# A decoder block on one core: gather by transposed matmuls in halves, branch pieces in another order, refills and stores by halves

## The chip, the cores and the metric

The program runs on one NeuronCore of a Trainium2 chip. The metric is the device time of one execution in microseconds (us). The engines are TensorE (PE; its weight loads are PEld), VectorE (DVE), ScalarE (ACT), GpSimd (POOL) and SyncE (SP), which here issues nearly all DMAs.

## The reference

One layer of a hybrid decoder with 256 tokens of width 1024, all in fp32:

```python
h = rms_norm(x, g_mix)
q, k, v, cb, cc, cx, ga, gc = split(h @ w_in + b_in)
y_attn = sliding_window_attention(rope(q), rope(k), v, sinks) @ w_attn_o
y_conv = (cb * causal_short_conv(cc * cx, w_conv)) @ w_conv_o
x = x + (sigmoid(ga) * y_attn + sigmoid(gc) * y_conv) @ w_out
h = rms_norm(x, g_ffn)
logits = h @ w_router + b_router            # 32 experts, top 4, softmax over them
for each expert e, for the tokens that chose it:
    g = minimum(h @ w_gate[e] + b_gate[e], 7);  u = clip(h @ w_up[e] + b_up[e], -7, 7)
    y += weight * ((g * sigmoid(1.702 * g) * (u + 1)) @ w_down[e] + b_down[e])
out = rms_norm(x + y, g_final)
```

## The kernel before

Weights come from memory once. The expert weights are 32 x 3 matrices of 4 MB. Each matrix is loaded as two runs of 2 MB, [128, 4096] fp32, into a ring of 10 slots; an expert takes six runs (gate, gate, up, up, down, down), 192 in all. SyncE issues the load of run p once run p-10 has been used (`weights_used`). A few loads, those in `HALVED`, go in two DMAs of 1 MB, so that the first half can be issued (`half_used`) or used (`half_full`) before the second. In the first stage the same memory holds pieces of 1 MB of the other matrices and intermediate results, so the first runs have to wait until those are spent.

**First stage.** A piece is 256 columns of a matrix. Its weights are split in a high part in fp32r (`wH`, by ScalarE, L925) and the rest (`wL`: by GpSimd for the first 128 columns, L1516, and by VectorE for the others, L1152), and TensorE adds three products. Pieces 0 to 25 are the input projection with attention and convolution. The eight branch pieces follow, in the order convolution 0, attention 0, convolution 1, attention 1 and so on. For each, ScalarE copies part of the PSUM result (`low_taken`), VectorE adds the rest (L1291) and multiplies by the gate (L1293, `branch_read`). After each attention piece VectorE adds both branches (L1296, `msum_ready`), ScalarE rounds the sum (L1008, `mH`), and VectorE takes the difference (L1298, `mL`, `merged_ready`). Then come four pieces of `w_out` (L511), which read `mH` and `mL`; the first does the products with rows 0 to 5 of them for both token tiles before it waits for the last `merged_ready`. On VectorE the low part for piece n+1 stands ahead of the work on the result of piece n.

**Experts.** For expert j, a one-hot matrix `Gr` picks up to 64 of the 256 tokens. `gather` multiplies it with `xres` to rows of tokens (L711), ScalarE copies these (`take_rows`, L1036), and four transposes (`turn_xe`, L719) give `xe`, the stationary operand of `wide`. `wide` runs over a matrix in 64-column tiles, two side by side (L746), after a bias matmul (L726). In TensorE's order an expert is: gate matrix, gather for j+1, up matrix, `turn_xe`, `scatter` of the expert before (L759, adds to the result in PSUM), transposes of the activation (L772) and of the combining weights (L766), down matrix. ScalarE's copy `take_act` (L1068) stands between the activation turn and the down matrix. The last two experts are interleaved: gate and up of both, then down of both. Banks 0 to 3 of PSUM hold the result, started by `residual` (L691). At the end VectorE and ScalarE do the final norm, and two stores write the output.

Of the kernel before, what the change touches and what calls it, by code (L numbers as in the profile page):

```python
# [61 lines left out]
HALVED = (EP, RING, NE * EP - 3, NE * EP - 1)  # L62
# [61 lines left out]
def hybrid_block(nc, A, out):  # L124
    ctx = ExitStack()
    with ctx:
# [85 lines left out]
        rows = work[:, 4096:4608]  # L212
# [15 lines left out]
        Gr = work[:, 4712:4840].rearrange("p (t c) -> p t c", t=TT)  # L228

# [45 lines left out]
        Gr_ready, rows_ready, xe_turned = sem("Gr_ready"), sem("rows_ready"), sem("xe_turned")  # L275
# [11 lines left out]
        out_ready = [sem(f"out_ready{t}") for t in range(TT)]  # L287
# [25 lines left out]
        def _(sp):  # L313
# [94 lines left out]
            def expert_turn(it, first):  # L408
                for c in range(UNROLL):
                    def wait(r, s):  # L410
                        p = c * EP + r
                        if first and p == RING and s == 0:
                            sp.wait_ge(half_used, 1)
                            return True
# [40 lines left out]
            for t in range(TT):  # L455
                sp.wait_ge(out_ready[t], 1)
                sp.dma_start(out[0, t * P:(t + 1) * P, :], normed[:, t, :]).then_inc(out_done, 16)
            sp.wait_ge(out_done, 16 * TT)
# [5 lines left out]
        def _(pe):  # L464
# [34 lines left out]
            def project(b, n, par, src, between=None, late=None, by_rows=None):  # L499
# [123 lines left out]
            for i in range(NKV):  # L623
                for src in (zz, aa):
# [46 lines left out]
            pe.wait_ge(merged_ready, NKV - 1)  # L671
            for i in range(NKV):
                if i == 3:
                    pe.wait_ge(x1_ready, 1)
                project((out_bank(i, 0), out_bank(i, 1)), n, n % 2, (mH, mL), None if i == 0 else lambda: turn_x1(i - 1),
                        (lambda: pe.wait_ge(merged_ready, NKV)) if i == 0 else None,
# [26 lines left out]
            residual(0, 1)  # L703
# [90 lines left out]
            def expert(j, c, uses):  # L794
# [15 lines left out]
                if not at(j, 0):  # L810
                    scatter(j, j)
# [770 lines left out]
```

## Time and profile before

| | |
|---|---|
| time, median of 3 runs | 1185.95 us (1185.67 to 1188.35) |
| the profiled execution's own time | 1186.93 us |
| its span, first to last instruction | 1185.2 us |
| TensorE busy | 1120.0 us, 95% |
| VectorE, ScalarE, GpSimd busy | 356.0, 227.4, 123.8 us |
| DMA moved | 447.63 MB, mean 378 GB/s |
| start of expert 0 on TensorE | 267.43 us |

Busy time of TensorE is no measure of its bound alone, since in the loop a transfer can end last while TensorE is busy for nine tenths. The stretches have different limits: what the transfers move, what TensorE waits for, and when one expert begins after the last have to be read for each. Times in rows are us from the start of the span. One fp32 matmul gives two records of matmul and two of weight load.

### The profile page before, as it was taken

How to read it: one execution, taken by the hardware profiler on the slowest of the kernel's cores; microseconds unless marked ns; L12 is line 12 of the kernel's file. 1: busy time of each engine (PE TensorE's matmuls, PEld its weight loads, DVE VectorE, ACT ScalarE, POOL GpSimd, SP SyncE). 2: the span in 40 equal slices, each digit the busy share in tenths (PEclk: the TensorE clock that was granted, in tenths of full speed). 3: DMA queues.
4: the chain of work that ended last, by engine and by line, in shares of the span. 5: the costliest groups of instructions: out<-in, count | busy, mean ns of one | idle time of the engine just before them, and what ended most of it. 6: DMA issues, size and time to landing. Idle time of an engine off the chain costs nothing.

```text
span 1185.2 us, 14843 instructions
## 1 busy us (share of the span) xinstructions
PE 1120.0 (95%) x5876; PEld 539.5 (46%) x5876; DVE 356.0 (30%) x623; ACT 227.4 (19%) x398; POOL 123.8 (10%) x94
## 2 busy tenths in 40 slices
PE   9899999999999999999999999999999999999896
PEld 7899998983333333333333333333333333333232
DVE  6967786842111111211111111111111111111121
ACT  5456656431001000100100000000000000000001
POOL 4453444420000000000000000000000000000000
PEclk9999999999999999999999998999999999999999
DMA  8454657899999999999999999999999999999994
GB/s 286 143 170 148 222 185 286 290 403 369 431 427 429 426 429 427 428 427 430 426 428 430 426 429 427 429 425 431 425 429 427 427 430 427 431 427 428 429 425 195
DMA packets 71836, 447.63 MB, mean 378 GB/s; under 512 B 5625, under 2 KB 45909, under 8 KB 46709
## 3 DMA queue, kind: packets, MB, share of 16 engines
q1 hardware_dynamic: 71520, 446.94, 91.7%
q8 instruction: 31, 0.51, 0.2%
q10 hardware_dynamic: 277, 0.12, 0.0%
q14 instruction: 8, 0.07, 0.0%
HBM read 445.59 MB, written 1.05 MB: 377 GB/s over the span
## 4 chain that ended last, share of the span: by engine, by line
PE 54%; DMA 34%; DVE 5%; issue 3%; ACT 2%; POOL 0%; SPq 0%; DVEq 0%; ACTq 0%; POOLq 0%
PE psum L746 33%; DMA ring<-in_w_up 29%; DMA ring<-in_w_down 4%; PE psum L759 4%; PE psum L477 3%; PE psum L491 3%; PE psum L711 2%; PE psum L772 1%; PE psum L481 1%; PE psum L495 1%; PE psum L719 1%; DMA ring<-in_w_out 1%; ACT work L1068 1%; DVE work L1293 1%; DVE work L1296 1%
## 5 line engine op out<-in xcount | busy, mean ns | idle before, releaser
L746 PE MATMUL psum<-ring,work 128*64 128x512 f32 x3072 | 687.5, 597 | 45.6 <-DMA ring<-in_w_gate 19.4
L746 PEld LDWEIGHTS psum<-ring,work 128*64 128x64 f32 x3072 | 215.8, 137 | 473.6 <-issue 380.2
L1377 DVE TENSOR_SCALAR work<-psum 128x512 f32<-128x512 f32 x32 | 22.1, 692 | 416.0 <-PE psum L746 416.0
L1516 POOL TENSOR_TENSOR w<-ring,w 128x1024 fp32r<-128x1024 f32 x38 | 101.2, 2668 | 108.7 <-ACT w L925 107.0
L1543 POOL COPY chosen<-pick 96x64 bf16 (+1 forms) x32 | 7.5, 235 | 872.1 <-PE psum L772 872.1
L1382 DVE TENSOR_SCALAR work<-psum 128x512 f32<-128x512 f32 x32 | 22.1, 692 | 226.0 <-PE psum L746 226.0
L1068 ACT COPY work<-psum 128x512 f32<-128x512 f32 x32 | 18.8, 586 | 332.2 <-PE psum L772 332.2
L1152 DVE TENSOR_TENSOR w<-ring,w 128x1024 fp32r<-128x1024 f32 x38 | 72.8, 1917 | 27.5 <-ACT w L925 27.1
L925 ACT CAST w<-ring 128x1024 fp32r<-128x1024 f32 x74 | 74.2, 1049 | 28.6 <-PE psum L481 15.8
L1077 ACT ACTIVATE work<-work 128x512 f32<-128x512 f32 x32 | 20.1, 630 | 256.7 <-DVE work L1377 256.7
L477 PE MATMUL psum<-hh,w 128*128 128x256 f32 x512 | 68.7, 288 | 0.0
L477 PEld LDWEIGHTS psum<-hh,w 128*128 128x128 f32 x512 | 65.0, 196 | 1.3 <-ACT w L925 1.3
L759 PE MATMUL psum<-work 64*128 64x512 f32 x256 | 63.6, 615 | 1.4 <-ACT work L1073 1.4
L1073 ACT COPY work<-psum 128x512 f32<-128x512 f32 x32 | 18.8, 586 | 230.1 <-PE psum L746 230.1
L711 PE MATMUL psum<-xres,work 128*64 128x512 f32 x256 | 60.4, 592 | 0.0
L1387 DVE COPY work<-psum 128x256 f32<-128x256 f32 x32 | 13.6, 424 | 78.4 <-PE psum L766 78.4
L481 PE MATMUL psum<-hh,w 128*128 128x256 f32 x256 | 35.9, 283 | 0.0
L711 PEld LDWEIGHTS psum<-xres,work 128*64 128x64 f32 x256 | 18.4, 137 | 36.7 <-issue 35.9
L481 PEld LDWEIGHTS psum<-hh,w 128*128 128x128 f32 x256 | 33.0, 192 | 0.0
L491 PE MATMUL psum<-hh,w 128*128 128x512 f32 x128 | 32.3, 394 | 0.6 <-issue 0.6
L759 PEld LDWEIGHTS psum<-work 64*128 64x128 f32 x256 | 22.0, 186 | 21.8 <-issue 15.1
L719 PEld LDWEIGHTS psum<-cst,work 128*128 128x128 f32 x128 | 17.9, 209 | 25.6 <-issue 25.2
(196 smaller groups left out, 804.4 us busy)
## 6 DMA issues: line engine op xcount, KB each, us to landing
ring<-in_w_up SPq DMA_DIRECT2D x64, 2048.0 KB, 40.8
ring<-in_w_gate SPq DMA_DIRECT2D x63, 2048.0 KB, 43.1
ring<-in_w_down SPq DMA_DIRECT2D x61, 2048.0 KB, 43.1
ring<-in_w_in SPq DMA_DIRECT2D x26, 1024.0 KB, 5.0
ring<-in_w_down SPq DMA_DIRECT2D x6, 1024.0 KB, 40.1
ring<-in_w_conv_o SPq DMA_DIRECT2D x4, 1024.0 KB, 5.1
ring<-in_w_attn_o SPq DMA_DIRECT2D x4, 1024.0 KB, 5.4
ring<-in_w_out SPq DMA_DIRECT2D x4, 1024.0 KB, 7.5
```

The lines of the kernel that those rows point to most:

```text
L477: pe.matmul(bank(b, m * T, T), wH[:, par, m, k, :], x[:, k, :], start=(k == 0 and x is low), stop=False)
L481: mm = pe.matmul(bank(b, m * T, T), wL[:, par, m, k, :], high[:, k, :], start=False, stop=(k == KB - 1))
L491: pe.matmul(bank(b[m]).rearrange("p (x t) -> p x t", x=2), wH[:, par, m, k, :], both[:, :, k, :], start=(k == 0), stop=(k == KB - 1))
L711: mm = pe.matmul(psum[64 * h:64 * h + 64, 6, :].rearrange("p (i r) -> p i r", r=RUN), Gr[:, t, :], x_runs[:, :, h, :], start=(t == 0), sto ...
L719: tr = pe.transpose(bank(6, r * P, P), rows.rearrange("p (i r) -> p i r", r=RUN)[:, :, r], ident)
L746: mm = pe.matmul(psum[64 * h:64 * h + 64, b, :], src[:, k, :], w[:, k2, h * 512:(h + 1) * 512], start=(bias_of is None and k == 0), stop=( ...
L759: pe.matmul(bank(2 * t + h), S[64 * h:64 * h + 64, t * P:(t + 1) * P], ysb[64 * h:64 * h + 64, :], start=False, stop=False, skip_group_che ...
L925: nc.scalar.copy(wH[:, par, m, :, :], slot(s).rearrange("p (k n) -> p k n", k=KB)[:, :, m * P:(m + 1) * P],).then_inc(wH_ready, rise if m ...
L1068: nc.scalar.copy(to.rearrange("p (h b) c -> p b h c", h=2), psum[:, 5, :].rearrange("p (b h c) -> p b h c", b=4, h=2)).then_inc(aT_ready, 1)
L1152: v.tensor_tensor(wL[:, p2, 1, :, :], slot(s).rearrange("p (k n) -> p k n", k=KB)[:, :, P:2 * P], wH[:, p2, 1, :, :].bitcast(F32), ALU.sub ...
L1377: v.tensor_scalar(gm, psum[:, 4, :], LIMIT, None, ALU.min).then_inc(gmin_ready, 1)
L1516: g.tensor_tensor(wL[:, par, 0, :, :], slot(s).rearrange("p (k n) -> p k n", k=KB)[:, :, 0:P], wH[:, par, 0, :, :].bitcast(F32), ALU.subtr ...
```

## The change

- `gather` is transposed: `xres` is now the stationary operand (every eighth number of a token tile, 128x128) and `Gr` the moving one (64 columns), so that the product is `xe` before its gain. 16 matmuls take the place of 4, and `take_rows`, `rows` and `turn_xe` are gone. It is cut in two halves of 8 matmuls: in an expert the first comes after the turns of activation and weights, the second between the two runs of the down matrix. In expert 0 the first half stands before the activation turn; for the last expert both stand after the up matrix of expert 30.
- The first gather compares the ranks in PSUM with the positions directly (`Mr0`), and goes to banks 6 and 5. The subtraction `below` comes after the mask. Two `residual` matmuls move into expert 1, and `turn_wgt` behind the first gate matrix.
- Branch pieces: convolution 0 to 3 first, then attention 0 to 3. The gated convolution result is kept in place of its gate. After every attention piece come sum, rounding and difference, in two buffers by turns. The first output piece takes rows 0 to 3, 4 to 5, 6 to 7, each behind its own `merged_ready`.
- Loads: run 3 is issued ahead of the output pieces instead of ahead of the third. Run 11 and the last four runs are loaded by halves.
- `turn_weights` of the last expert moves between the two runs of the down matrix of expert 30. The final norm works by quarters, with four stores.

```diff
-HALVED = (EP, RING, NE * EP - 3, NE * EP - 1)
+HALVED = (EP, RING, RING + 1, NE * EP - 4, NE * EP - 3, NE * EP - 2, NE * EP - 1)
...
-            tail += [w[:, :, i * PW:(i + 1) * PW] for i in range(NKV) for w in (w_co, w_ao)]
+            tail += [w[:, :, i * PW:(i + 1) * PW] for w in (w_co, w_ao) for i in range(NKV)]
...
-                if n == NP1 - 2:
-                    sp.wait_ge(blocks_done, 2 * (NIN + 2 * NKV - 1))
+                if n == NIN + 2 * NKV:
+                    sp.wait_ge(blocks_done, 2 * (NIN + NKV))
                     load_run(0, 3, 3)
...
                 if late is not None:
-                    for t in range(TT):
-                        block(t, range(KB - 2))
-                    late()
+                    for blocks in range(2):
+                        for t in range(TT):
+                            block(t, range((KB - 4) * blocks, KB - 4 + 2 * blocks))
+                        late(NKV - 1 + blocks)
...
-            def gather(nth):
+            def gather(nth, halves=range(RUNS), banks=(6, 6)):
 
                 pe.wait_ge(Gr_ready, nth + 1)
-                for t in range(TT):
-                    x_runs = xres[:, t, :].rearrange("p (i h r) -> p i h r", h=RUNS, r=RUN)
-                    for h in range(RUNS):
-                        mm = pe.matmul(psum[64 * h:64 * h + 64, 6, :].rearrange("p (i r) -> p i r", r=RUN), Gr[:, t, :],
-                                       x_runs[:, :, h, :], start=(t == 0), stop=(t == TT - 1), tile_position=(0, 64 * h))
-                mm.then_inc(gathered, 1)
-
-            def turn_xe(nth):
-
-                pe.wait_ge(rows_ready, nth + 1)
-                for r in range(RUN):
-                    tr = pe.transpose(bank(6, r * P, P), rows.rearrange("p (i r) -> p i r", r=RUN)[:, :, r], ident)
-                tr.then_inc(xe_turned, 1)
+                for h in halves:
+                    for k in range(RUN * h, RUN * h + RUN):
+                        for t in range(TT):
+                            mm = pe.matmul(bank(banks[h], k * CW, CW), xres[:, t, :].rearrange("p (i k) -> p i k", k=KB)[:, :, k],
+                                           Gr[:, t, :], start=(t == 0), stop=(t == TT - 1))
+                    if banks[0] != banks[1] and h == 0:
+                        mm.then_inc(half_gathered, 1)
+                if RUNS - 1 in halves:
+                    mm.then_inc(gathered, 1)
...
                 turn_act(j)
                 turn_weights(j)
+                if not at(j, 0):
+                    gather(j + 1, range(1))
                 pe.wait_ge(aT_ready, j + 1)
                 if not at(j, 0):
                     pe.wait_ge(ysb_ready, j)
-                wide(7, aT, c * EP + 2 * RUNS, uses, None, base)
+                wide(7, aT, c * EP + 2 * RUNS, uses, None, base, lambda: gather(j + 1, range(1, RUNS)))
...
+                if nth < NKV:
+                    v.tensor_tensor(flat(theirs), summed, flat(theirs), ALU.mult).then_inc(branch_read, 1)
+                    continue
+                if nth == 2 * NKV - 1:
+                    dve.wait_ge(merged_ready, NKV - 2)
+                v.tensor_tensor(flat(tmp), summed, flat(ours), ALU.mult).then_inc(branch_read, 1)
+                dve.wait_ge(branch_read, nth + 1)
+                v.tensor_tensor(flat(tmp), flat(tmp), flat(theirs), ALU.add).then_inc(msum_ready, 1)
                 dve.wait_ge(mH_ready, i + 1)
-                v.tensor_tensor(mL[:, 2 * i:2 * i + 2, :], raw, mH[:, 2 * i:2 * i + 2, :].bitcast(F32),
+                v.tensor_tensor(mL[:, 2 * i:2 * i + 2, :], tmp, mH[:, 2 * i:2 * i + 2, :].bitcast(F32),
                                 ALU.subtract).then_inc(merged_ready, 1)
```

VectorE before, from the low part ahead of the last but one branch piece's result to the low part for the second output piece (`w2` is the split weights, `mt` and `normed` the gates of attention and convolution):

```order
L1152 TENSOR_TENSOR w2_54<-ring,w2_54 128x1024 [waits wH_ready,merged_ready]
L1291 TENSOR_TENSOR work<-psum,work 128x512 [waits low_taken,blocks_done]
L1293 TENSOR_TENSOR work<-work,normed_49 128x512 [waits dve_step]
L1152 TENSOR_TENSOR w2_54<-ring,w2_54 128x1024 [waits wH_ready]
L1293 TENSOR_TENSOR work<-psum,mt_50 128x512 [waits blocks_done]
L1296 TENSOR_TENSOR work<-work 128x512 [waits branch_read]
L1298 TENSOR_TENSOR mL_56<-work,mH_55 128x512 [waits mH_ready]
L1152 TENSOR_TENSOR w2_54<-ring,w2_54 128x1024 [waits wH_ready,merged_ready]
```

VectorE now, at the same place (L1149 is the low part of the weights, L1297 the sum, L1299 the difference):

```order
L1149 TENSOR_TENSOR w2_54<-ring,w2_54 128x1024 [waits wH_ready]
L1286 TENSOR_TENSOR work<-psum,work 128x512 [waits low_taken,blocks_done]
L1295 TENSOR_TENSOR work<-work,mt_50 128x512 [waits dve_step]
L1297 TENSOR_TENSOR work<-work,normed_49 128x512 [waits branch_read]
L1299 TENSOR_TENSOR mL_56<-work,mH_55 128x512 [waits mH_ready]
L1149 TENSOR_TENSOR w2_54<-ring,w2_54 128x1024 [waits wH_ready]
L1295 TENSOR_TENSOR work<-psum,mt_50 128x512 [waits merged_ready,blocks_done]
L1297 TENSOR_TENSOR work<-work,normed_49 128x512 [waits branch_read]
L1299 TENSOR_TENSOR mL_56<-work,mH_55 128x512 [waits mH_ready]
L1149 TENSOR_TENSOR w2_54<-ring,w2_54 128x1024 [waits wH_ready,merged_ready]
```

The second low part in each list is the one for the first output piece. Between it and the multiplication before it now stand a sum and a difference, the latter behind ScalarE's rounding.

TensorE before, in an expert, from the end of the up matrix to the down matrix's second run:

```order
L719 MATMUL psum<-cst,work 128x128 [waits rows_ready]
L719 MATMUL psum<-cst,work 128x128 x3
L759 MATMUL psum<-work 128x512 [waits S_ready,ysb_ready]
L759 MATMUL psum<-work 128x512 x3
L772 MATMUL psum<-cst,work 128x128 [waits act_ready]
L772 MATMUL psum<-cst,work 128x128 x3
L766 MATMUL psum<-cst,work 128x128 [waits Gw_ready]
L766 MATMUL psum<-cst,work 128x128
L746 MATMUL psum<-ring,work 64x512 [waits slot_full0,ysb_ready,aT_ready]
L746 MATMUL psum<-ring,work 64x512 x7
L746 MATMUL psum<-ring,work 64x512 [waits slot_full6]
L746 MATMUL psum<-ring,work 64x512 x7
```

TensorE now, at the same place (L713 is the gather; L757, L770, L764 and L744 are scatter, both turns and `wide`):

```order
L757 MATMUL psum<-work 128x512 [waits S_ready,ysb_ready]
L757 MATMUL psum<-work 128x512 x3
L770 MATMUL psum<-cst,work 128x128 [waits act_ready]
L770 MATMUL psum<-cst,work 128x128 x3
L764 MATMUL psum<-cst,work 128x128 [waits Gw_ready]
L764 MATMUL psum<-cst,work 128x128
L713 MATMUL psum<-work,xres 128x64 [waits Gr_ready]
L713 MATMUL psum<-work,xres 128x64 x7
L744 MATMUL psum<-ring,work 64x512 [waits slot_full0,ysb_ready,aT_ready]
L744 MATMUL psum<-ring,work 64x512 x7
L713 MATMUL psum<-work,xres 128x64 [waits Gr_ready]
L713 MATMUL psum<-work,xres 128x64 x7
```

The turn of the gathered rows is gone, and half a gather stands on either side of the down matrix's first run; the old gather between gate and up matrix is gone as well.

## Rows read from the trace of the kernel before

**Rows 1.** The page, part 4: the chain that ended last, by engine.

```profile
PE 54%; DMA 34%; DVE 5%; issue 3%; ACT 2%; POOL 0%; SPq 0%; DVEq 0%; ACTq 0%; POOLq 0%
```

**Rows 2.** Stretches: length, busy us of PE, PEld, DVE, ACT, POOL; clock; DMA; GB/s.

```profile
186.00:231.00 45.00, 44.98 (x275) 40.31 (x274) 38.09 (x31) 23.47 (x36) 19.57 (x8) 1.00 0.86 303
267.40:300.00 32.60, 31.28 (x150) 12.08 (x152) 6.97 (x22) 3.76 (x6) 0.23 (x1) 1.00 0.97 376
300.00:600.00 300.00, 294.82 (x1406) 107.24 (x1404) 54.41 (x123) 27.49 (x46) 2.58 (x11) 1.00 1.01 428
600.00:1122.00 522.00, 483.12 (x2246) 168.76 (x2242) 85.21 (x196) 41.78 (x70) 4.22 (x18) 0.99 1.01 428
720.00:740.00 20.00, 19.75 (x72) 7.25 (x70) 3.43 (x9) 1.17 (x2) 0.24 (x1) 0.83 1.01 428
```

**Rows 3.** TensorE timeline, one expert: start us, busy us, what [idle before].

```profile
302.16 0.39 PE L726 MATMUL psum<-bias,chosen 96*64 96x512 bf16 x2
...
309.35 0.75 PE L719 MATMUL psum<-cst,work 128*128 128x128 f32 x4
310.02 1.99 PE L759 MATMUL psum<-work 64*128 64x512 f32 x8
...
313.37 7.09 PE L746 MATMUL psum<-ring,work 128*64 128x512 f32 x32 [0.46 <-ACT work L1068]
...
327.37 1.89 PE L711 MATMUL psum<-xres,work 128*64 128x512 f32 x8
329.09 0.39 PE L726 MATMUL psum<-bias,chosen 96*64 96x512 bf16 x2
```

**Rows 4.** TensorE timeline: the down bias, and two late waits for landings.

```profile
724.20 4.37 PE L788 MATMUL psum<-cst,wT 32*128 32x512 f32 x8
...
1122.03 5.35 PE L746 MATMUL psum<-ring,work 128*64 128x512 f32 x16 [2.43 <-DMA ring<-in_w_gate]
...
1156.32 3.65 PE L746 MATMUL psum<-ring,work 128*64 128x512 f32 x16 [1.10 <-DMA ring<-in_w_down]
```

**Rows 5.** Timeline of weight loads: routing, contiguous transposes, strided transposes.

```profile
242.98 0.98 PEld L653 LDWEIGHTS psum<-wr,work 128*128 128x128 f32 x8
...
239.69 0.46 PEld L640 LDWEIGHTS psum<-cst,xres 128*128 128x128 f32 x4
...
757.57 0.56 PEld L772 LDWEIGHTS psum<-cst,work 128*128 128x128 f32 x4 [0.76 <-issue]
```

**Rows 6.** Timeline of GpSimd, VectorE and TensorE around the first output piece.

```profile
228.04 2.40 POOL L1516 TENSOR_TENSOR w<-ring,w 128x1024 fp32r<-128x1024 f32 x1 [4.40 <-ACT w L925]
228.18 2.80 DVE L1293 TENSOR_TENSOR work<-work,normed 128x512 f32<-128x512 f32 x1
230.91 1.21 DVE L1152 TENSOR_TENSOR w<-ring,w 128x1024 fp32r<-128x1024 f32 x1
...
234.13 0.69 DVE L1298 TENSOR_TENSOR mL<-work,mH 128x512 fp32r<-128x512 f32 x1 [0.69 <-ACT mH L1008]
...
230.98 0.28 PE L511 MATMUL psum<-w,mL 128*128 128x256 f32 x1
```

**Rows 7.** Timeline from the ranks to expert 0, VectorE and TensorE.

```profile
262.55 0.23 DVE L1349 SCALAR_TENSOR_TENSOR pos<-psum,Mb 128x64 f32<-128x64 f32 x1 [0.46 <-PE psum L702]
...
263.41 1.94 PE L711 MATMUL psum<-xres,work 128*64 128x512 f32 x8
265.27 1.12 PE L691 MATMUL psum<-xres,cst 128*128 128x512 f32 x2
...
267.43 0.41 PE L726 MATMUL psum<-bias,chosen 96*64 96x512 bf16 x2 [0.34 <-issue]
```

**Rows 8.** SyncE's queue: the first refill, two halves.

```profile
269.59 2.04 SPq L341 DMA_DIRECT2D ring<-in_w_down  x2
```

**Rows 9.** TensorE timeline, between expert 30 and expert 31.

```profile
1136.11 0.75 PE L719 MATMUL psum<-cst,work 128*128 128x128 f32 x4
...
1140.85 0.41 PE L726 MATMUL psum<-bias,chosen 96*64 96x512 bf16 x2 [1.18 <-DVE work L1400]
```

More of the change, by code:

```diff
@@ L228, in hybrid_block @@
         Gr = work[:, 4712:4840].rearrange("p (t c) -> p t c", t=TT)
+        Mr0 = work[:, 4994:4996]
         posT = work[0:NE, 4096:4096 + T]
@@ L286, in hybrid_block @@
         gfin_in, x2g_ready, out_done = sem("gfin_in"), sem("x2g_ready"), sem("out_done")
-        out_ready = [sem(f"out_ready{t}") for t in range(TT)]
+        out_ready = [[sem(f"out_ready{t}{h}") for h in range(2)] for t in range(TT)]
         def pieces(w):
@@ L411, in wait @@
                         p = c * EP + r
-                        if first and p == RING and s == 0:
-                            sp.wait_ge(half_used, 1)
+                        if first and p in (RING, RING + 1) and s == 0:
+                            sp.wait_ge(half_used, p + 1 - RING)
                             return True
@@ L455, in _ @@
             for t in range(TT):
-                sp.wait_ge(out_ready[t], 1)
-                sp.dma_start(out[0, t * P:(t + 1) * P, :], normed[:, t, :]).then_inc(out_done, 16)
-            sp.wait_ge(out_done, 16 * TT)
+                for h in range(2):
+                    sp.wait_ge(out_ready[t][h], 1)
+                    sp.dma_start(out[0, t * P:(t + 1) * P, h * 512:(h + 1) * 512],
+                                 normed[:, t, h * 512:(h + 1) * 512]).then_inc(out_done, 16)
+            sp.wait_ge(out_done, 16 * 2 * TT)
         @block.tensor
@@ L622, in _ @@
             n = NIN
-            for i in range(NKV):
-                for src in (zz, aa):
+            for src in (zz, aa):
+                for i in range(NKV):
                     if n >= NIN + 3:
@@ L804, in expert @@
                 wide(4, xe, c * EP, uses, 0, base)
-                gather(j + 1)
+                if at(j, 0):
+                    turn_wgt()
+                if at(j, 1):
+                    residual(0, 1)
+                    residual(1, 1)
+                wide(5, xe, c * EP + RUNS, uses, 1, base)
                 if at(j, 0):
                     pe.wait_ge(wT_ready, 1)
-                wide(5, xe, c * EP + RUNS, uses, 1, base)
-                turn_xe(j + 1)
-                if not at(j, 0):
+                    gather(j + 1, range(1))
+                else:
                     scatter(j, j)
@@ L815, in expert @@
                 turn_weights(j)
+                if not at(j, 0):
+                    gather(j + 1, range(1))
                 pe.wait_ge(aT_ready, j + 1)
@@ L1019, in _ @@
                     split_high(n + 1, (n + 1) % RING1, 16 * ((n + 1) // RING1 + 1), (n + 1) % 2)
-                i, second = (n - NIN) // 2, (n - NIN) % 2
-                if i and not second:
-                    sum_high(i - 1)
-                if not second:
+                nth = n - NIN
+                if nth > NKV:
+                    sum_high(nth - NKV - 1)
+                if nth < 2:
                     act_e.wait_ge(rotated, NKV + 1)
-                    if i:
-                        act_e.wait_ge(merged_ready, i)
+                elif nth < NKV + 2:
+                    act_e.wait_ge(branch_read, nth - 1)
+                else:
+                    act_e.wait_ge(merged_ready, nth - NKV - 1)
                 if n < NIN + 2 * NKV - 1:
@@ L1095, in _ @@
             squash(a)
-            take_rows(b)
             take_act(a)
@@ L1114, in _ @@
                                      accum_out=small[:, 44 + b:45 + b]).then_inc(ssq_ready, 1)
-            act_e.wait_ge(rstd_ready, RSTD0 + 1)
-            act_e.wait_ge(x2g_ready, 2)
-            nc.scalar.activation(normed[:, 0, :], normed[:, 0, :], ACT.Copy, scale=small[:, 52:53]).then_inc(out_ready[0], 1)
+            for t, h in ((0, 0), (0, 1), (1, 0)):
+                act_e.wait_ge(rstd_ready, RSTD0 + t + 1)
+                act_e.wait_ge(x2g_ready, 2 * t + h + 1)
+                done = normed[:, t, h * 512:(h + 1) * 512]
+                nc.scalar.activation(done, done, ACT.Copy, scale=small[:, 52 + t:53 + t]).then_inc(out_ready[t][h], 1)
         @block.vector
@@ L1274, in _ @@
             flat = lambda x: x.rearrange("p m t -> p (m t)")
-            for i in range(NKV):
-                if i:
-                    dve.wait_ge(merged_ready, i)
-                if i == 1:
+            for nth in range(2 * NKV):
+                i, tmp = nth % NKV, (raw, swp)[nth % 2]
+                if nth == 2:
                     dve.wait_ge(bias_cut, 1)
                     v.tensor_tensor(bias, bias, bcut[:, 0, :, :], ALU.subtract).then_inc(bias_rest, 1)
-                if i == 2:
+                if nth == 4:
                     dve.wait_ge(bias_cut, 2)
@@ L1352, in one_hot @@
             def one_hot(nth, table, at):
-                if not (isinstance(nth, int) and nth == 0):
-                    dve.wait_ge(gathered, nth)
+                dve.wait_ge(gathered, nth)
                 for t in range(TT):
```

98 lines of the change are left out of this document (41 added, 57 removed).

## The prediction

> **What bounds the kernel now.** I read the chain of waits first: TensorE holds 54% of it and DMA 34% [rows 1], so one rule does not cover the whole span. The table by stretches then splits it [rows 2]. From 186 to 231 us, the branch pieces, TensorE is busy 44.98 of 45.00 us: whatever makes it wait there is paid in full. From 300 to 600 us DMA moves 428 GB/s at full share, and it moves the same from 600 to 1122 us, so that is its ceiling; between 267.4 and 300 us it reaches 376. TensorE is busy 294.82 of 300 us in the first of these stretches and 483.12 of 522 in the second. Two speeds lie behind that. The TensorE timeline of one expert early in the loop runs from bias to bias in 329.09 - 302.16 = 26.93 us, with no wait for data [rows 3]. The transfers need more: TensorE waited for a landing until 1122.03 and again until 1156.32, and seven runs (a run is 2 MB, half a matrix, six to an expert) lie between, so one lands every 4.90 us and an expert every 29.4 us [rows 4]. The first ten runs stand ready when the experts start, so TensorE runs at its own pace, gains 2.4 us per expert on the transfers, and waits for them from about the middle on. The time is thus: start of expert 0 (267.43) + ramp of the transfers + 29.4 us per expert + tail, as long as TensorE needs under 29.4 less what the ten ready runs leave.
>
> **Part 1, the gather.** Removed per expert: the four gather matmuls, 329.09 - 327.37 = 1.72 us, and the four transposes, 310.02 - 309.35 = 0.67 us; the wait of 0.46 us before the down matrix now has half a gather ahead of it and goes [rows 3]. That leaves 24.08. Added: 16 matmuls of 128x128 weights with 64 moving columns, each two records, so 32 loads of full weights. No such load from `xres` at a step of eight numbers is in the trace. Nearest are the routing matmuls, fp32, contiguous: eight loads take 0.98 us, of which the last lasts 0.19, so (0.98 - 0.19)/7 = 0.113 each; columns are not what limits them. Four contiguous transposes load in 0.46 us, four at a step of four numbers (activation turn) in 0.56 [rows 5]. The step so costs between 0 and 0.10/4 = 0.025 per load. Bounds: 0.113 and 0.140 each, the latter with the turn's whole 0.56 divided by four. I take 0.1225, the contiguous load plus 0.010, since the excess is partly the last load's own length: 3.9 us. With 0.1 to 0.2 for changing between 64-column tiles and full ones, an expert needs 28.1 us (bounds 27.7 and 28.7).
>
> Is 28.1 hidden? From the start of expert 0 to the end of the fourth run of expert 30 TensorE then has 30 x 28.1 = 843.0, the two residual matmuls moved into expert 1, 2.2 (1.1 each, [rows 7]), the spreading of the down bias 4.4 [rows 4], the half-speed stretch behind it 3.4 (granted 0.83 of full over the 20 us from 720 on, [rows 2]), less 2.0 for the scatter that expert 0 lacks, plus twice 309.35 - 302.16 = 7.2 for four runs [rows 3]: 865.4. The transfers set this point at: landing of its second run 1122.0 - 267.4 = 854.6 after the start, two runs more 9.8, last half pass 3.5, less the ramp's 1.8 (below): 866.1. The two are within 1 us. So the gather is hidden, but its cover is used up: each further 0.1 us per expert costs 3 us.
>
> In the last pair it is not hidden. Between the fourth run of expert 30 (1136.11) and the bias of expert 31 (1140.85) lie 4.74 us [rows 9]; there 0.67 goes [rows 3] and both halves of a gather come, 3.9 + 0.3: +3.5. Against that, TensorE waited 1.10 us later for a landing (until 1156.32, [rows 4]), which is now covered, -1.1, and it entered this stretch 0.8 late (1136.1 against 1122.0 + 9.8 + 3.5), which came from the old gather and from 5.35 us for 16 matmul records behind a wait of 2.43 us, granted 1.2 GHz: -0.8. Loading the last runs by halves brings nothing more, since TensorE is behind them. Sum +1.6.
>
> **Part 2, the refills.** Expert 0's second run now frees its slot by halves, and the third is freed 1.7 us sooner (no gather between). Before, the two halves of the first refill were issued from 269.59 on, within 2.04 us [rows 8], and the next only once the second run was wholly used, some 3.5 us later; DMA had run dry. DMA lost (1 - 376/428) x 32.6 = 4.0 us up to 300 [rows 2]; that bounds the gain, 0 below. Half of the second refill can be issued half a pass over a run, 3.5/2 = 1.75 us, sooner, so I take 1.8. The 2 MB run moved ahead of the output pieces lands earlier, but the ring is full before expert 0 either way: 0. The first output piece now queues behind it and could land up to 4.9 us later [rows 4]; ScalarE rounds that piece only at the end of the branch pieces, which hides it. Without that cover the 4.9 us would be TensorE's.
>
> **Part 3, branch pieces and output.** TensorE does the same work in another order and has no wait to give back. VectorE has. Before, after the last but one piece it multiplied (228.18, 2.80 us because GpSimd's 2.40 from 228.04 ran beside it), and at once made the low part of the first output weights, L1152, done at 232.12. The sum, the rounding by ScalarE and the difference, 0.69 + 0.69 + 0.69, came behind (one such operation takes 0.69, and VectorE waited 0.69 for ScalarE) [rows 6]. The order shown above has these three now ahead of it. Its end moves by 2.1 to 234.2. TensorE begins the first output piece at 230.98, one matmul per weight load (0.113 to 0.12 us, [rows 5]); it now wants that low part after 8 matmuls instead of 12, at 231.9. It waits 2.3 us, in the open, with everything on it. The finer waits for `merged_ready` give nothing, because no wait was there. Bounds: 0 if VectorE gets ahead, 4.0 if it also gives up its turn to GpSimd once and TensorE falls to 1.2 GHz behind the wait (1.7 more, as 5.35 against 3.65 in [rows 4]).
>
> **Part 4, the first gather.** The first gather's positions are compared straight in PSUM: the one-hot loses the step before it (0.23, [rows 7]), and a subtraction of the same size leaves the path ahead of the mask: -0.4. From 263.41 to 267.43 the path was gather, residual, turns [rows 7]; now gather 3.9 and 0.2 of change. Sum -0.3 (bounds -0.8 and +0.8).
>
> **Part 5, the stores.** Two stores of 512 KB become four of half the size. The last is ready some 0.3 us sooner and moves 256 KB instead of 512, 0.6 us at 428 GB/s: -0.9 (0 to -1.3).
>
> **Sum**: +1.6 - 1.8 + 2.3 - 0.3 - 0.9 = +0.9 on the profiled execution, 1186.93, so 1187.8. That execution lies 1.0 above the median of 1185.95, so 1186.9; I say **1187**.
>
> **Rivals.** A difference of 0.3% (3.6 us) is about what a measurement of this kernel can tell from none.
> - *Forecast*, hidden gather and late low part, 1183.5 to 1189.5: 0.48.
> - *TensorE becomes the bound.* At 28.3 us per expert 3 to 6 us are added, 1190 to 1193; at the upper bound of 28.7, 0.55 x 30 = 16 us, 1204. For it speaks that the cover is below 1 us; against it that the step costs little in [rows 5]. 0.30.
> - *Strided weights load far more slowly.* If a step of eight costs twice what a step of four does at most, 0.05 per load, an expert takes 24.08 + 32 x 0.163 + 0.15 = 29.4 us: +37 us, 1224. 0.08.
> - *Faster.* If VectorE is not late (-2.3) and the ramp gives back all 4.0 instead of 1.8, 1182.5. [rows 6] shows no time to spare between VectorE's operations. 0.08.
> - *No effect*: if DMA sets everything after the start and VectorE's delay is refilled by the ramp, 1186. Inside the first range: 0.06.
>
> The Trainium skill's page Advanced Engine Details and Errata, section SBUF Cachelines, says that SBUF lines are 16 bytes, and that reads which hit a new line each time pay a penalty. It speaks against this change: `xres` read every eighth fp32 number is a new line per weight. It gives no figure. In the trace the transposes at a step of 16 bytes load four in 0.56 us instead of 0.46, so the trace agrees on the sign; by the row the kernel stays near 1187, by a penalty that grows with the step it is the third case.
>
> **The numbers.** Chances: faster by over 0.3% 0.08, within 0.54, slower 0.38. Range: it leaves out the faster case below and the third case above, and takes in the second's bound: 1183.5 to 1205; the forecast's own range is 1183.5 to 1189.5.
>
> **What would show it.** The TensorE timeline of an early expert: 28.1 us from bias to bias, the new gather 1.9 to 2.1 us per half, no wait for ScalarE before the down matrix. TensorE idle about 2.3 us near 232, ended by VectorE's L1149. Expert 0 starting near 269.4. Waits for landings only in the last experts. 428 GB/s reached sooner after the start. The prediction is wrong if the period differs from 28.1 by over 0.2, if DMA falls below 428 GB/s in mid-loop, or if TensorE has no gap at 232.

## Result: 13% slower, and the profile after

The changed kernel takes 1344.98 us (1343.67 to 1345.88, 4 runs), the kernel before 1185.98: a ratio of 1.1335, 95% interval [1.1315, 1.1355]. The prediction was 1187, range 1183.5 to 1205.

The page of the changed kernel: the busy line, and the chain that ended last.

```profile
PE 1324.8 (99%) x6516; PEld 759.2 (56%) x6516; DVE 355.4 (26%) x592; ACT 209.7 (16%) x368; POOL 125.1 (9%) x94
...
PE 93%; DVE 4%; issue 2%; ACT 1%; DVEq 0%; POOL 0%; ACTq 0%; POOLq 0%
```

DMA has left the chain, where it held 34% [rows 1]; TensorE now holds 93% of it. The table by stretches of the changed kernel says the same (busy time of each engine, granted clock, DMA share, GB/s):

```profile
186.00:231.00 45.00, 44.95 (x273) 40.09 (x272) 35.91 (x29) 22.91 (x35) 20.94 (x8) 1.00 0.93 323
267.40:300.00 32.60, 32.35 (x134) 16.96 (x133) 5.95 (x17) 2.86 (x4) 0.23 (x1) 0.84 0.76 308
300.00:600.00 300.00, 300.00 (x1318) 147.65 (x1317) 43.59 (x90) 16.24 (x27) 2.11 (x9) 0.96 0.91 376
600.00:1122.00 522.00, 522.00 (x2286) 256.90 (x2288) 75.69 (x157) 28.28 (x47) 3.51 (x15) 0.95 0.91 375
```

In [rows 2] the two long stretches moved 428 GB/s. Now TensorE is busy all the time, DMA moves 376 and 375, and the granted clock is 0.96 and 0.95. The TensorE timeline of one expert of the changed kernel, from bias to bias, answers to [rows 3]:

```profile
377.48 0.39 PE L724 MATMUL psum<-bias,chosen 96*64 96x512 bf16 x2
377.70 7.04 PE L744 MATMUL psum<-ring,work 128*64 128x512 f32 x32
...
391.76 1.99 PE L757 MATMUL psum<-work 64*128 64x512 f32 x8
393.68 0.75 PE L770 MATMUL psum<-cst,work 128*128 128x128 f32 x4
394.26 0.38 PE L764 MATMUL psum<-cst,work 128*128 128x128 f32 x2
394.48 3.92 PE L713 MATMUL psum<-work,xres 128*128 128x64 f32 x16
398.33 3.65 PE L744 MATMUL psum<-ring,work 128*64 128x512 f32 x16
401.92 4.03 PE L713 MATMUL psum<-work,xres 128*128 128x64 f32 x16
405.87 5.35 PE L744 MATMUL psum<-ring,work 128*64 128x512 f32 x16
411.05 0.39 PE L724 MATMUL psum<-bias,chosen 96*64 96x512 bf16 x2
```

The expert takes 411.05 - 377.48 = 33.57 us. Two things are new. Each half of the gather (L713) takes 3.9 us where 1.9 to 2.1 was forecast. And 16 records of the down matrix take 5.35 us behind the second half, 3.65 behind the first: the granted clock fell. The windows of the changed kernel one expert earlier show the fall (busy time, clock, DMA share, GB/s):

```profile
360.92:364.76 3.84, 3.84 (x18) 1.00 1.02 435
364.76:370.05 5.29, 5.29 (x18) 0.68 1.00 424
370.05:374.00 3.95, 3.95 (x19) 1.00 0.76 257
374.00:377.48 3.48, 3.48 (x17) 1.00 0.72 306
```

While the gather runs the clock is full; in the matrix behind it the mean is 0.68, so part of it ran at 1.2 GHz instead of 2.4. Of the 30 intervals from expert to expert up to expert 30, eight take 31.87 us, without such a stretch. The other 22 hold at least one, and one costs 1.70 us.

Where the 158.9 us of the two profiled spans (1344.1 and 1185.2) lie: expert 0 starts at 272.72 instead of 267.43, +5.3; from there to the start of expert 30 it is 1002.2 us instead of 848.3, +153.9; the rest is 0.3 shorter. At the start the changed kernel shows the first gather and the bias behind it, which answer to [rows 7]:

```profile
264.89 7.90 PE L713 MATMUL psum<-work,xres 128*128 128x64 f32 x32 [0.72 <-DVE work L1352]
272.72 0.64 PE L724 MATMUL psum<-bias,chosen 96*64 96x512 bf16 x2
```

Near 232 stands the forecast wait of TensorE, of 1.62 us instead of 2.3. The timelines of TensorE and VectorE of the changed kernel there:

```profile
233.92 0.36 PE L513 MATMUL psum<-w,mH 128*128 128x256 f32 x1 [1.62 <-DVE w L1149]
...
228.35 2.18 DVE L1295 TENSOR_TENSOR work<-work,mt 128x512 f32<-128x512 f32 x1
230.57 0.69 DVE L1297 TENSOR_TENSOR work<-work,normed 128x512 f32<-128x512 f32 x1
231.95 0.69 DVE L1299 TENSOR_TENSOR mL<-work,mH 128x512 fp32r<-128x512 f32 x1 [0.69 <-ACT mH L1011]
232.55 1.22 DVE L1149 TENSOR_TENSOR w<-ring,w 128x1024 fp32r<-128x1024 f32 x1
```

The low part (L1149) stands behind the sum and the difference, as the prediction said, and ends at 233.77 instead of 232.12 [rows 6].

### The profile page after: what moved, and what is told of

Read it like the earlier page. It is cut to its first block, busy times and chain, and to the rows that moved or that the text cites. A ratio compares the mean times of both kernels' runs of the same rounds, so it can differ in the third digit from the quotient of the medians.

```text
span 1344.1 us, 16068 instructions
## 1 busy us (share of the span) xinstructions
PE 1324.8 (99%) x6516; PEld 759.2 (56%) x6516; DVE 355.4 (26%) x592; ACT 209.7 (16%) x368; POOL 125.1 (9%) x94
## 3 DMA queue, kind: packets, MB, share of 16 engines
HBM read 445.59 MB, written 1.05 MB: 332 GB/s over the span
## 4 chain that ended last, share of the span: by engine, by line
PE 93%; DVE 4%; issue 2%; ACT 1%; DVEq 0%; POOL 0%; ACTq 0%; POOLq 0%
PE psum L744 53%; PE psum L713 18%; PE psum L757 5%; PE psum L493 3%; PE psum L479 3%; PE psum L513 2%; PE psum L497 2%; PE psum L770 2%; PE psum L483 1%; PE psum L724 1%; DVE w L1149 1%; PE psum L764 1%; PE psum L563 0%; DVE work L1295 0%; DVE work L1250 0%
## 5 line engine op out<-in xcount | busy, mean ns | idle before, releaser
L744 PE MATMUL psum<-ring,work 128*64 128x512 f32 x3072 | 724.6, 623 | 0.2 <-ACT work L1068 0.2
L744 PEld LDWEIGHTS psum<-ring,work 128*64 128x64 f32 x3072 | 224.1, 143 | 428.0 <-issue 418.4
L713 PEld LDWEIGHTS psum<-work,xres 128*128 128x128 f32 x1024 | 248.7, 334 | 26.8 <-issue 26.0
L713 PE MATMUL psum<-work,xres 128*128 128x64 f32 x1024 | 254.4, 404 | 0.7 <-DVE work L1352 0.7
L1396 DVE TENSOR_TENSOR work<-psum,g2k 128x512 f32<-128x512 f32 x31 | 21.4, 692 | 345.1 <-PE psum L713 345.1
L1149 DVE TENSOR_TENSOR w<-ring,w 128x1024 fp32r<-128x1024 f32 x38 | 77.7, 2046 | 26.3 <-ACT w L928 26.0
L757 PE MATMUL psum<-work 64*128 64x512 f32 x256 | 65.2, 629 | 1.4 <-ACT work L1073 1.4
L757 PEld LDWEIGHTS psum<-work 64*128 64x128 f32 x256 | 22.5, 190 | 42.4 <-issue 39.2
L770 PEld LDWEIGHTS psum<-cst,work 128*128 128x128 f32 x128 | 18.1, 211 | 24.2 <-DVE work L1387 21.2
```

Source lines behind the costliest of these rows:

```text
L713: mm = pe.matmul(bank(banks[h], k * CW, CW), xres[:, t, :].rearrange("p (i k) -> p i k", k=KB)[:, :, k], Gr[:, t, :], start=(t == 0), stop ...
L744: mm = pe.matmul(psum[64 * h:64 * h + 64, b, :], src[:, k, :], w[:, k2, h * 512:(h + 1) * 512], start=(bias_of is None and k == 0), stop=( ...
L757: pe.matmul(bank(2 * t + h), S[64 * h:64 * h + 64, t * P:(t + 1) * P], ysb[64 * h:64 * h + 64, :], start=False, stop=False, skip_group_che ...
L770: tr = pe.transpose(bank(5, b * P, P), act_runs[:, b // RUN, :, b % RUN], ident)
L1149: v.tensor_tensor(wL[:, p2, 1, :, :], slot(s).rearrange("p (k n) -> p k n", k=KB)[:, :, P:2 * P], wH[:, p2, 1, :, :].bitcast(F32), ALU.sub ...
```

## Experiments

### Which part holds the loss

**The old gather back, everything else kept.** Edit: the transposed gather's lines undone.

> The changed kernel with the gather of before (four matmuls with xres moving, ScalarE's copy, four transposes, at their old places); refills and last runs by halves, the branch order, the first output piece in three steps, the first one-hot straight from PSUM and the four stores are kept. Theory (the whole loss is the gather): 1184 to 1188 us, with TensorE's wait of 1.6 us near 232 us still there and the ramp and the stores giving it back. Rival (the slower part is also in the refills, or the halves cost DMA rate): the loop's DMA stays under 428 GB/s and the kernel takes over 1200 us.

Measured: 1186.55 us, ratio 1.0001 [0.9992, 1.0010]; TensorE's wait near 232 is 1.6 us, DMA 428 GB/s in both long stretches. The parts other than the gather move nothing in sum that can be measured. The ramp does not give the wait back, as the theory had it: DMA moves 374 GB/s there, 376 before [rows 2].

**The gather alone** on the kernel before.

> The kernel before with the transposed gather alone (first gather and first one-hot included); refills, branch pieces, last runs and stores as before. Theory: 1343 to 1348 us, all of the loss. Rival (the gather only hurts together with the halved refills or the moved loads): under 1330 us.

Measured: 1344.13 us, ratio 1.1325 [1.1303, 1.1348]. The gather is the whole loss, and the theory holds from both sides.

### What makes the gather slow

**Contiguous weights.** Edit in `gather`:

```
- xres[:, t, :].rearrange("p (i k) -> p i k", k=KB)[:, :, k]
+ xres[:, t, k * P:(k + 1) * P]
```

> The changed kernel with one edit: the gather loads its weights from xres as 128 neighbouring fp32 numbers instead of every eighth. It so gathers other columns than the reference wants; count, size and place of every instruction stay. Theory (the step of 32 bytes is what costs): one load again every 0.113 to 0.123 us instead of 0.238, a gather of 3.6 to 3.9 us instead of 7.6, an expert of 27.8 to 28.1 us, TensorE at 2.4 GHz before the down matrix, the kernel at 1185 to 1192 us. Rival (count: 32 loads of 128 columns with only 64 moving columns behind each cost this in any layout): 0.238 us each, 1345 us. Second rival (the half-speed stretches behind the gather come from its narrow matmuls and not from its length): 16 matmul records behind a half gather still take 5.35 us instead of 3.65 in two of three experts, an expert of 29.2 us, 1195 to 1205 us.

Measured: 1186.47 us, ratio 1.0001 [0.9991, 1.0011]. TensorE timeline of that run: the first gather, then in a later expert both halves of the gather, each with the half of the down matrix behind it:

```profile
265.18 3.79 PE L713 MATMUL psum<-work,xres 128*128 128x64 f32 x32 [0.72 <-DVE work L1352]
...
342.67 1.90 PE L713 MATMUL psum<-work,xres 128*128 128x64 f32 x16
344.49 3.65 PE L744 MATMUL psum<-ring,work 128*64 128x512 f32 x16
348.08 2.00 PE L713 MATMUL psum<-work,xres 128*128 128x64 f32 x16
350.00 3.65 PE L744 MATMUL psum<-ring,work 128*64 128x512 f32 x16
```

Its windows, with the columns as above:

```profile
267.40:300.00 32.60, 32.14 (x177) 14.22 (x177) 7.42 (x22) 3.44 (x5) 0.23 (x1) 1.00 0.99 406
300.00:600.00 300.00, 300.00 (x1574) 130.08 (x1570) 51.62 (x105) 19.22 (x32) 2.56 (x11) 1.00 1.01 427
600.00:1122.00 522.00, 513.30 (x2671) 219.56 (x2671) 88.81 (x185) 32.99 (x55) 4.19 (x18) 1.00 1.01 428
```

With the same instructions in the same places, an expert takes 27.82 us, the clock is 1.00, and the 1.2 GHz stretches behind the gathers are gone. Both rivals, count and narrow matmuls, fall. In time this is the kernel that was predicted, though it gathers the wrong columns: 1186.5 us against 1187, 27.82 us against 28.1.

**The price by step.** Edit: block `k` loads at a step of `k + 1` numbers.

```
+ xres[:, t, 0:(P - 1) * (k + 1) + 1:k + 1]
```

> The changed kernel with one edit: the four loads of block k of the gather read xres at a step of k + 1 numbers, so that steps of 4, 8, 12 ... 32 bytes stand side by side in each gather. Other columns are gathered than the reference wants. Theory A (each new 16-byte line costs the same): the load's price rises to a step of four numbers and stays there, so the steps 4 to 8 all take about 0.24 us. Theory B (the price grows with the distance read): a step of four costs 0.12 as the activation turn's row suggests, and 5 to 8 rise from there to 0.24. Theory C (only a step of exactly 32 bytes or a power of two is bad, for instance banks): 3, 5, 6, 7 cost as little as 1, and 8 costs 0.24. By B the gather takes some 5.3 us and an expert 29.5; the kernel 1190 to 1230 us; by A 6.5 us and 1280 us.

Measured: 1270.84 us, ratio 1.0708 [1.0688, 1.0727]. TensorE's weight loads of that run; each row is a block of four, at steps of 1, 2, 3, 4, 5, 6, 7 and 8 numbers in this order (start, us from the first start to the last end):

```profile
477.13 0.53 PEld L713 LDWEIGHTS psum<-work,xres 128*128 128x128 f32 x4
477.58 0.55 PEld L713 LDWEIGHTS psum<-work,xres 128*128 128x128 f32 x4
478.05 0.78 PEld L713 LDWEIGHTS psum<-work,xres 128*128 128x128 f32 x4
478.74 1.02 PEld L713 LDWEIGHTS psum<-work,xres 128*128 128x128 f32 x4
483.41 0.96 PEld L713 LDWEIGHTS psum<-work,xres 128*128 128x128 f32 x4 [0.81 <-issue]
484.27 0.99 PEld L713 LDWEIGHTS psum<-work,xres 128*128 128x128 f32 x4
485.17 1.02 PEld L713 LDWEIGHTS psum<-work,xres 128*128 128x128 f32 x4
486.09 1.05 PEld L713 LDWEIGHTS psum<-work,xres 128*128 128x128 f32 x4
```

Theory A holds in shape: 0.53 and 0.55 us for four loads at steps of one and two numbers, a part of the price at three, all of it at four (16 bytes), and nearly level from there. From start to start a load takes 0.112 us at a step of one and 0.238 at eight. B, which the prediction's bound rested on, falls at step four: 1.02 us, not 0.56. C falls as well, since five, six and seven cost as much as eight. The total lies under the 1280 us that A gave.

The Trainium skill, page Advanced Engine Details and Errata, section SBUF Cachelines, adds to its 16-byte lines that at least two hits on a line are needed to hide the access. By that rule a step of two numbers costs nothing and a step of four all of it. The trace agrees, with 0.55 against 1.02 us.

**Longer steps, a shifted start, and transposes.** Edit: the gather's blocks at steps of 1, 4, 1 (begun one number later), 9, 10, 12, 14 and 16, the four activation transposes at 2, 4, 8 and 16, all from `xres`.

> The changed kernel with other columns gathered and other numbers turned than the reference wants. The eight blocks of the gather load at steps of 1, 4, 1 (begun one number later), 9, 10, 12, 14 and 16 numbers; the four activation transposes load from xres at steps of 2, 4, 8 and 16. Theory (a new 16-byte line per number costs the same at any distance): loads of matmuls 0.112, 0.233, 0.112 and then all 0.22 to 0.24 us; transposes 0.11 for a step of 2 and the same 0.12 for 4, 8 and 16, because a transpose has time to spare in each load. Rival (the price goes on growing with the step, as 0.222, 0.225, 0.231 and 0.238 us for 5 to 8 may say): about 0.29 us at 16, and transposes at 8 and 16 well over 0.12. Second rival (transposes pay as much as matmuls once the step passes four): 0.22 us and more for the turns at 8 and 16. The kernel between 1310 and 1345 us.

Measured: 1290.91 us, ratio 1.0883 [1.0863, 1.0903]. The weight loads of that run: a shifted start, then steps of 12 and of 16, and last the four transposes:

```profile
512.51 0.54 PEld L718 LDWEIGHTS psum<-work,xres 128*128 128x128 f32 x4
...
518.53 1.16 PEld L718 LDWEIGHTS psum<-work,xres 128*128 128x128 f32 x4
...
520.57 0.96 PEld L718 LDWEIGHTS psum<-work,xres 128*128 128x128 f32 x4
...
510.46 0.55 PEld L775 LDWEIGHTS psum<-cst,xres 128*128 128x128 f32 x4 [0.76 <-DVE work L1392]
```

A shifted start costs nothing, twelve is the dearest of the steps tried (1.16 us), sixteen is cheaper than eight (0.96), so the price neither grows with distance nor follows powers of two; that twelve is dearer was in no theory. The total of 1291 lies under the 1310 expected. The last row is the one that explains the error: transposes at steps of 2, 4, 8 and 16 load four in 0.55 us together, as at four in [rows 5] (0.56), against 0.46 contiguous. A transpose hardly pays for the step, at any length tried; an fp32 matmul pays double. Why the two differ, no run shows.

**A correct kernel with contiguous loads.** Edit: gate and up matrices fetched by row blocks, so that the gather may read neighbouring columns.

```
- A[n].rearrange("l e (p h r) n -> (l e) p h r n", p=P, r=RUN)
+ A[n].rearrange("l e (h r p) n -> (l e) p h r n", p=P, r=RUN)
- xres[:, t, :].rearrange("p (i k) -> p i k", k=KB)[:, :, k]
+ xres[:, t, k * P:(k + 1) * P]
```

> The changed kernel with contiguous gather loads and the reference's result: the gather reads blocks of 128 neighbouring columns of xres, the gate and up matrices are fetched with row k * 128 + p on partition p (four pieces of 4 KB per partition and run instead of one of 16 KB), and the gain comes from the copy that already has this order. Theory (stride is all that was wrong, and transfers keep their rate at 4 KB pieces): loads every 0.112 us, DMA at 428 GB/s from 300 to 1122 us, 1184 to 1189 us. Rival (4 KB pieces move slower): DMA under 420 GB/s in the same stretch, TensorE waits for landings of gate and up from the start, over 1200 us.

Measured: 1210.86 us, ratio 1.0208 [1.0194, 1.0221]. Windows of that run:

```profile
300.00:600.00 300.00, 300.00 (x1568) 129.33 (x1566) 51.59 (x105) 19.73 (x33) 2.56 (x11) 1.00 1.02 415
600.00:1122.00 522.00, 500.65 (x2560) 212.87 (x2558) 83.91 (x175) 31.19 (x52) 3.96 (x17) 0.99 1.02 415
```

The gather is as fast as expected and an expert takes 27.82 us, but DMA moves 415 GB/s instead of 428: the rival on transfers is right in its rate and in the time. TensorE does not wait from the start, though, but, as before, from the middle on. The stride is cured at the price of some 25 us of transfers. The edit makes the pieces smaller and also changes their order in memory, and no run separates the two.

### Why the clock falls

**The strided gather dealt out by fours.** Edit: in the up and the down matrix, behind each of eight blocks `k`:

```
+ if each is not None:
+     each(k)   # four loads of the gather
```

> The changed kernel with the strided gather of experts 1 to 30 dealt out by fours: after each of the last four blocks of the up matrix and of the first four of the down matrix stand four of its 32 loads, instead of two stretches of sixteen. Theory (TensorE falls to 1.2 GHz because a stretch of sixteen strided loads leaves it 3.9 us with few columns moved): granted clock 0.99 to 1.00 from 300 to 1122 us instead of 0.95 and 0.96, no matmul block at 1.2 GHz; an expert of 31.9 us plus 8 changes of tile instead of 2 at 0.1 us, so 32.0 to 32.8, and the kernel 1305 to 1335 us. Rival (what counts is how much strided loading an expert holds, wherever it stands): the clock stays at 0.95 and the kernel takes 1345 us or more.

Measured: 1381.87 us, ratio 1.1651 [1.1630, 1.1672]. TensorE timeline of that run:

```profile
356.25 1.17 PE L712 MATMUL psum<-work,xres 128*128 128x64 f32 x4
357.35 1.08 PE L754 MATMUL psum<-ring,work 128*64 128x512 f32 x4
358.36 1.16 PE L712 MATMUL psum<-work,xres 128*128 128x64 f32 x4
...
367.00 1.08 PE L754 MATMUL psum<-ring,work 128*64 128x512 f32 x4 [0.46 <-ACT work L1083]
```

On the clock the theory holds: 0.99 and 1.00 instead of 0.96 and 0.95, so it is unbroken stretches of slow loads that precede the fall, not their number in an expert. A long stretch is not followed by it each time: the run with steps of 1 to 8 has 4.0 us of strided loads without a break in nearly every expert and 1.2 GHz in 8 of the 30 intervals, the changed kernel in 22. Nor is the stride alone the cause. The first gather of the contiguous run, 3.79 us without a break, leaves the clock at 1.00. But in the kernel before, the clock fell in the down bias, 4.37 us of matmuls without a strided load [rows 4] (0.83 from 720 to 740 us [rows 2]). What decides whether it falls stays open.

On the total the theory missed. An expert takes 34.35 us, 2.48 more than 31.87. The wait of 0.46 us for ScalarE before the down matrix is back, since no half gather stands ahead of it any more. The six more groups between wide matmuls take the other 2.0 us, 0.34 us each for two changes of tile, not 0.1 (an estimate from these differences). The rival's "1345 us or more" came true, but not for its reason, the clock. Spreading is worse than the fall it avoids.

### The rest of the change

**The branch order alone**, with the output piece in three steps and run 3 moved ahead.

> The kernel before with the new order of branch pieces, the first output piece in three steps and the load of run 3 moved ahead of the output pieces, alone. Theory: TensorE waits 1.6 us for VectorE's low part near 232, expert 0 starts 1.2 to 1.6 us later than in before, the kernel 1 to 1.7 us over before. Rival (the ring is fuller at the later start, and the transfers take it back): expert 0 later by as much, but the kernel within 0.5 us of before.

Measured: 1187.71 us, ratio 1.0014 [1.0005, 1.0023], expert 0 at 268.38. The theory held in the total, a small loss of 1.35 us between the medians, and in the wait of 1.6 us. Expert 0 starts 0.95 us later than before, less than the 1.2 to 1.6 expected.

**All but the branch order and the gather.**

> The kernel before with its own gather and its own order of branch pieces, and these parts of the change: second refill by halves, last four runs by halves, first one-hot straight from PSUM, last turn of the weights earlier, four stores. Theory (the branch order's wait of 1.6 us took away what the others give): no wait near 232, expert 0 starts at 267.1 to 267.4, the kernel 0.5 to 2 us under before, 1184.2 to 1185.7. Rival (the transfers set everything behind the start, so the rest gives nothing): within 0.5 us of before.

Measured: 1185.04 us, ratio 0.9990 [0.9982, 0.9999]: the only version that is faster than before, by 1.3 us between the medians. Its expert 0 starts at 266.12, but the whole profile stands 0.9 us earlier from 160 us on, where the code is the same; the start alone so proves 0.4 us at most.

**The low part first**: all of the change but the gather, and VectorE's low part put ahead of the sum (its old place, one piece later, is left empty; only the added lines are shown).

```
+ if nth == 2 * NKV - 2:
+     split_low(n + 1, None)
```

> All of the change but the gather, as in the run with the old gather, and one edit more: VectorE makes the low part of the first output weights right behind the multiplication of the last but one branch piece, ahead of its sum and its difference, as in the order of before. Theory (TensorE's wait near 232 is this low part being late behind those two): no wait of TensorE there, expert 0 starts 1.6 us sooner after the last branch piece than in the run with the old gather, 1184.5 to 1185.5 us against 1186.5. Rival (the sums are then late in its place): TensorE waits as long for the difference of the same piece, 1186 to 1187 us.

Measured: 1186.87 us, ratio 1.0006 [0.9997, 1.0015]. The waits of TensorE from 228 to 262 us in that run (us in total, times, longest):

```profile
PE psum L514 <- DVE mL L1317: 0.8, 1, 0.8
PE psum L514 <- DVE w L1164: 0.3, 1, 0.3
```

VectorE's timeline there, with the low part (L1164) ahead of the sum (L1315):

```profile
230.28 1.21 DVE L1164 TENSOR_TENSOR w<-ring,w 128x1024 fp32r<-128x1024 f32 x1
231.41 0.68 DVE L1315 TENSOR_TENSOR work<-work,normed 128x512 f32<-128x512 f32 x1
```

The wait for the first low part is gone, and waits for the last difference (L1317) and for the next low part stand in its place. The theory had the cause of the wait right and its cure wrong: in this order VectorE has a sum, a wait for ScalarE's rounding and a difference more to do ahead of the output pieces, and something is late wherever they stand. The rival's total came true; the difference that TensorE waits for is that of the last piece, not of the one before.

**The first one-hot alone.**

> The kernel before with one part: the first one-hot compared straight in PSUM and the subtraction moved behind the mask. Theory: from VectorE's L1335 to the first gather matmul 2.8 us instead of 3.05, the kernel 0.1 to 0.4 us under before. Rival (the transfers set the time behind the start): no difference in the total.

Measured: 1186.16 us, ratio 0.9998 [0.9989, 1.0007]; from that operation of VectorE to the first gather it is 2.81 us instead of 3.05. A gain of 0.24 is seen in the profile and not in the total.

**The halved refill and last runs alone.**

> The kernel before with one part: refill of the second run and the last four runs loaded by halves. Theory (an earlier refill starts the transfers earlier): DMA 381 GB/s instead of 376 from 267.4 to 300 us, the kernel 0.5 to 1.0 us under before. Rival (nothing in the ramp is missing at the end): within 0.2 us of before.

Measured: 1185.19 us, ratio 0.9992 [0.9983, 1.0001]. DMA moves 375 GB/s from 267.4 to 300, no more than before, so the reason given is wrong. In the last pair the waits for landings are 0.35 and 0.29 us where before had 1.10 [rows 4]. The gain of about 1.3 us is at the edge of what the runs can tell (the interval reaches 1.0001), and its place is not settled.

## Why the prediction was wrong, step by step

**The step that failed** is the price of the strided load in part 1: "I take 0.1225", with 0.113 and 0.140 as bounds. It is 0.238. The upper bound came from the four activation transposes of [rows 5], and the runs show that transposes are no measure for an fp32 matmul: at a step of four, four loads take 0.56 us in the one and 1.02 in the other. The row gave a bound only for its own kind of instruction. 32 x (0.238 - 0.1225) = 3.7 us per expert: 28.1 becomes 31.8, and the intervals without a fall of the clock show 31.87.

The trace of before held a stronger hint than the merged row. The loads one by one (ns: shortest, median, longest), the activation turn at a step of four and a contiguous turn:

```profile
L772 PEld LDWEIGHTS psum<-cst,work x4: 196/212/220, 757.6 to 757.9; 128*128 128x128 f32 x4
L640 PEld LDWEIGHTS psum<-cst,xres x7: 138/140/143, 239.7 to 247.0; 128*128 128x128 f32 x7
```

From start to start the step hardly shows, since these loads overlap, but one load lasts half as long again. In the changed kernel one load of the gather lasts 0.335 us, in the contiguous run 0.192.

**The rival "strided weights load far more slowly"** named the mechanism, at a chance of 0.08 and 1224 us. Its size was off because it doubled the same transposes' excess: 0.163 per load and 29.4 us instead of 0.238 and 31.87. The sentence on 16-byte lines was the better guide than the row weighed against it.

**A term was missing**: the clock. 22 of the 30 intervals hold 1.2 GHz, which costs 1.70 us in most of them. The sum can be made against the contiguous run, which takes 850.3 us from expert 0 to expert 30. The stride adds 30 x (31.87 - 27.82) = 121.5. What the 22 intervals take beyond that is 41.3 us, counted interval by interval. The first has 4.8 of it: behind the first gather of 7.90 us its granted clock is 0.85. The waits for landings, with which the contiguous run's last seven intervals take 29.4 instead of 27.8 us, go: -11. That gives 1002, and the changed kernel takes 1002.2. The contiguous run and the spread one show that here this fall goes away with the stride, and also with the unbroken stretch.

**Right**: the table of what bounds the kernel, the 24.08 us that are left without the old gather, and hiding a gather of 3.9 us under the transfers (contiguous run, 1186.5). The cover was as thin as the prediction said: at 27.82 us per expert 11 us of waits for landings are left in 30 intervals, and 0.28 us more in each, up to the forecast 28.1, would take 8.4 of them. Part 3 was right in mechanism and sign, 1.62 us instead of 2.3: the low part ended 1.65 us later, not 2.1, since the multiplication ahead of it took 2.18 us instead of 2.80. Part 4's one-hot was right in kind, with 0.24 instead of 0.4; its gather took 7.8 us instead of 3.9, by the same wrong price. Part 2's gain in the ramp does not come from the halved refill, with which the ramp moves 375 GB/s where before moved 376. With the contiguous gather it moves 406, so some 2.3 us of transfers come earlier there (30/428 of 32.6 us, an estimate), near the 1.8 forecast; that they come from the third slot's earlier release is likely and not shown. "Loading the last runs by halves brings nothing more" was said for the new gather, and no run tests it there. The last pair's +1.6 and part 5, the stores, were not tested apart. The sum of everything but the gather, forecast near zero, measured a ratio of 1.0001.

## What to carry to other kernels

Before the stationary side of an fp32 matmul is given a stride, look how many numbers it skips: here a step of two was free (0.55 us for four loads), and from four on, when each number lies 16 bytes or more behind the last, a load took twice as long, 0.238 us instead of 0.112. A bound from the trace holds for the same instruction only: a transpose's load was another kind than a matmul's, even with the same shape, type and step. Look at single loads, too, and not only at merged rows. Where no row shows it, change the columns read and nothing else, as the contiguous run did: that one edit splits layout from everything else in one run. And where a term uses up the cover of the bound beside it, the range must reach as far as its price can go, times the number of turns.

## What was unexpected of the hardware

- The price of a stride for fp32 matmul weights, for four loads: 0.53 and 0.55 us at steps of one and two numbers, 0.78 at three, 1.02 at four, 0.96 to 1.05 from five to eight, 1.16 at twelve, 0.96 at sixteen. Transposes: 0.55 at steps of 2, 4, 8 and 16 together, 0.46 contiguous.
- TensorE at 1.2 GHz behind 3.9 us of strided loads without any idle time: the matmuls are counted as busy, and the granted clock of the matrix behind them is 0.68. It does not come behind every such stretch (22 of 30 intervals). Behind 1.9 and 3.79 us of contiguous ones it stays at 1.00.
- With gate and up matrices in pieces of 4 KB instead of 16 KB, and in another order in memory, DMA moves 415 GB/s instead of 428, at a DMA share of 1.02: 3% of the rate, 25 us of this kernel.
- A group of four weight loads of 128 columns between 64-column tiles costs about 0.3 us beside its own loads (an estimate from the spread run).
